# Attention's second product with the values' two halves side by side in one stationary operand

## The reference, cut to what matters

```
proj = rmsnorm(x) @ w_in            # sparse q,k,v | indexer | stick-breaking q,k,v | gates
o_a  = sparse attention             # 8 heads of 64: top-128 keys by the indexer, T5 bias, softmax
o_b  = stick-breaking attention     # 8 heads of 64, strictly causal
m    = sigmoid(gate_a) * (o_a @ W_a) + sigmoid(gate_b) * (o_b @ W_b)
x    = x + rmsnorm(m @ w_out);  x = x + rmsnorm(SwiGLU(rmsnorm(x)) @ w_down)
```

## Time and profile before

| | us |
|---|---|
| median of 3 runs | 823.9 (822.6 to 826.22) |
| the profiled execution | 822.08 |
| its span, first to last instruction | 820.3 |
| PE busy | 798.2 |
| DVE, ACT, POOL busy | 383.6, 325.7, 406.0 |

### The profile page before, as it was taken

The page is one execution under the profiler, slowest core; times in us unless marked ns, Lnnn a source line. Parts: engine busy times, 40 slices in busy tenths (PEclk is TensorE's granted clock), DMA queues, the critical chain, the costliest instruction groups (busy, mean ns, idle before and its releaser), DMA issues.

```text
span 820.3 us, 10762 instructions
## 1 busy us (share of the span) xinstructions
PE 798.2 (97%) x3822; PEld 663.4 (81%) x3822; DVE 383.6 (47%) x539; ACT 325.7 (40%) x472; POOL 406.0 (49%) x246
## 2 busy tenths in 40 slices
PE   6999999999999899999999999999999999999996
PEld 5887888888888788788878988888888888888885
DVE  4359996687686766349707300000000020444464
ACT  5463322656656565543136322222222232232242
POOL 4276464544476867434455234444444443443462
PEclk9999999999999999999999999999999999999999
DMA  7323333223222222223267033233333332232212
GB/s 221 101 52 94 138 116 102 68 58 81 52 54 63 58 59 78 64 78 102 103 219 218 1 101 84 81 92 102 102 102 102 102 102 80 74 102 102 102 52 103
DMA packets 103913, 77.29 MB, mean 94 GB/s; under 512 B 3777, under 2 KB 95945, under 8 KB 103882
## 3 DMA queue, kind: packets, MB, share of 16 engines
q1 hardware_dynamic: 103882, 76.87, 31.6%
HBM read 74.75 MB, written 3.68 MB: 96 GB/s over the span
## 4 chain that ended last, share of the span: by engine, by line
PE 90%; DMA 3%; ACT 2%; DVE 1%; issue 1%; POOL 1%; SPq 0%; ACTq 0%; POOLq 0%
PE ps L435 20%; PE ps L407 20%; PE ps L409 20%; PE ps L408 19%; PE ps L628 4%; PE ps L617 2%; DMA raw<-in_w_gate_up 2%; PE ps L598 1%; PE ps L596 1%; DMA raw<-in_w_in 1%; POOL w_lo L1044 1%; DMA raw<-in_w_out 1%; ACT w_hi L738 1%; DVE h_lo L1188 0%; PE ps L527 0%
## 5 line engine op out<-in xcount | busy, mean ns | idle before, releaser
L1044 POOL TENSOR_TENSOR w_lo<-raw,w_hi 128x1024 fp32r<-128x1024 f32 x116 | 281.9, 2430 | 341.6 <-ACT w_hi L738 312.2
L407 PE MATMUL ps<-h_hi,w_hi 128*128 128x512 f32 (+1 forms) x656 | 252.7, 385 | 8.9 <-issue 3.0
L738 ACT ACTIVATE w_hi<-raw 128x1024 fp32r<-128x1024 f32 (+1 forms) x111 | 117.6, 1059 | 338.5 <-PE ps L409 229.0
L409 PE MATMUL ps<-h_hi,w_lo 128*128 128x512 f32 (+1 forms) x656 | 249.2, 380 | 0.0
L408 PE MATMUL ps<-h_lo,w_hi 128*128 128x512 f32 (+1 forms) x656 | 248.7, 379 | 0.0
L407 PEld LDWEIGHTS ps<-h_hi,w_hi 128*128 128x128 f32 x656 | 123.5, 188 | 32.8 <-issue 4.9
L409 PEld LDWEIGHTS ps<-h_hi,w_lo 128*128 128x128 f32 x656 | 123.4, 188 | 24.1
L408 PEld LDWEIGHTS ps<-h_lo,w_hi 128*128 128x128 f32 x656 | 123.6, 188 | 21.3
L1421 DVE TENSOR_TENSOR act<-silu,ps 128x512 f32 (+1 forms) x22 | 15.1, 688 | 211.2 <-PE ps L409 211.2
L1426 DVE TENSOR_TENSOR d_lo<-act,d_hi 128x512 fp32r<-128x512 f32 x18 | 43.2, 2404 | 54.1 <-ACT d_hi L986 54.1
L435 PE MATMUL ps<-w_lo,d_hi 128*128 128x512 f32 x144 | 45.4, 396 | 0.0
(11 more groups left out here) (179 smaller groups left out, 1216.4 us busy)
## 6 DMA issues: line engine op xcount, KB each, us to landing
raw<-in_w_in SPq DMA_DIRECT2D x44, 512.0 KB, 4.8
raw<-in_w_gate_up SPq DMA_DIRECT2D x44, 512.0 KB, 4.9
raw<-in_w_down SPq DMA_DIRECT2D x22, 512.0 KB, 3.9
raw<-in_w_out SPq DMA_DIRECT2D x8, 512.0 KB, 3.9
x_in<-in_x SPq DMA_DIRECT2D x4, 512.0 KB, 5.7
raw<-in_w_branch_sb SPq DMA_DIRECT2D x8, 256.0 KB, 3.1
raw<-in_w_branch_sparse SPq DMA_DIRECT2D x8, 256.0 KB, 3.2
x<-in_x SPq DMA_DIRECT2D x4, 512.0 KB, 8.2
```

Source lines behind the costliest of these rows:

```text
L407: mm(acc, whi_c, a_hi_, start=first, stop=False)
L409: return mm(acc, wlo_c, a_hi_, start=False, stop=last)
L738: run(w_hi[:, at(u), :], raw[:, at((d % 2) * 2 + u), :], ACT.Copy).then_inc(w_hi_done, 1)
L1044: nc.gpsimd.tensor_tensor(w_lo[:, at(u), :], raw[:, at((d % 2) * 2 + u), :], w_hi[:, at(u), :], sub).then_inc(w_lo_done, 1)
```

## The change

The two heads of a pair get a stationary operand each, 128 wide: the 64 columns of the head's `v_hi`, and beside them the 64 of its `v_lo` (`v_both[:, head, block, :]`). Two passes, over `a_hi` and over `a_lo`, give `v_hi`·a in PSUM rows 0 to 63 and `v_lo`·a in rows 64 to 127. (The product lo·lo, left out before, is now included.) The result of the head is the sum of the two parts. ScalarE copies the lower part to SBUF, to the rows where the head's result does not belong (`out_rest`), VectorE adds the upper part from PSUM into the rows where it does (`sum_out`), and from there `out_hi` and `rest_out` make the halves.

The order changes with it. `turn_probs(i+1)` waits for `out_summed` of head i. `out_hi(i-1)` stands behind `turned_hi(i)` on ScalarE. `rest_out(i-1)` stands ahead of `sum_out(i)` on VectorE. `out_rest(i)` on ScalarE stands where `out_hi(i)` stood and, because `out_parts` has one buffer, waits for `o_lo_done` of head i-1 too. Two small tiles move to memory that is used otherwise later.

```
@@ attend, on TensorE
-                for p, (v, pr) in enumerate(((v_hi, a_hi), (v_hi, a_lo), (v_lo, a_hi))):
-                    ins = mm(z(1, k * P, S), v[:, k, :], pr[:, a:a + n],
-                             start=k == 0 and p == 0, stop=k == TB - 1 and p == 2, skip_group_check=True)
+                for p, pr in enumerate((a_hi, a_lo)):
+                    ins = mm(z(1, k * P, S), v_both[:, i % 2, k, :], pr[:, a:a + n],
+                             start=k == 0 and p == 0, stop=k == TB - 1 and p == 1, skip_group_check=True)
@@ turn_probs
-                pe.wait_ge(o_lo_done, i)
+                pe.wait_ge(out_summed, i)
@@ split_v: the same number of elements, now in runs of 64
-            run(v_hi[:, :, :], v_tok[:, :, first:first + P], ACT.Copy).then_inc(v_hi_done, 1)
+            run(v_both[:, :, :, 0:HD], v_tok[:, :, first:first + P].rearrange("p t (h d) -> p h t d", h=2),
+                ACT.Copy).then_inc(v_hi_done, 1)
@@ ScalarE
+        def out_rest(i):
+            r = slice(HD * (i % 2), HD * (i % 2) + HD)
+            sc.wait_ge(out_done, i + 1)
+            other = slice(HD - r.start, P - r.start)
+            if i:
+                sc.wait_ge(o_lo_done, i)
+            run(out_parts[other, :], ps[HD:P, 5, :], ACT.Copy).then_inc(out_rest_done, 1)
         def out_hi(i):
-            sc.wait_ge(out_done, i + 1)
-            run(o_hi[r:r + HD, chunk, :], ps[r:r + HD, 5, :], ACT.Copy).then_inc(o_hi_done, 1)
+            sc.wait_ge(out_summed, i + 1)
+            run(o_hi[r, chunk, :], out_parts[r, :], ACT.Copy).then_inc(o_hi_done, 1)
@@ ScalarE, step i
             turned_hi(i)
+            if i:
+                out_hi(i - 1)
...
-            out_hi(i)
+            out_rest(i)
...
+        out_hi(ALL - 1)
@@ VectorE
+        def sum_out(i):
+            r = slice(HD * (i % 2), HD * (i % 2) + HD)
+            ve.wait_ge(out_rest_done, i + 1)
+            other = slice(HD - r.start, P - r.start)
+            tt(out_parts[r, :], ps[0:HD, 5, :], out_parts[other, :], ALU.add).then_inc(out_summed, 1)
         def rest_out(i):
-            tt(o_lo[r, chunk, :], ps[r, 5, :], o_hi[r, chunk, :], sub).then_inc(o_lo_done, 1)
+            tt(o_lo[r, chunk, :], out_parts[r, :], o_hi[r, chunk, :], sub).then_inc(o_lo_done, 1)
@@ VectorE, step i
-            rest_out(i)
+            if i:
+                rest_out(i - 1)
+            sum_out(i)
+        rest_out(ALL - 1)
```

More of the change, by code:

```diff
@@ L149, in build @@
     rel_t = sb("rel_t", BUCKETS, rows=HEADS)
-    f_bias = sb("f_bias", 384, rows=HEADS)
-    zeros8 = sb("zeros8", 384, rows=HEADS)
     zone1 = top[0]
@@ L165, in build @@
     q_lo = sb("q_lo", [2, S], F32R)
-    v_hi, v_lo = sb("v_hi", [TB, P], F32R), sb("v_lo", [TB, P], F32R)
+    v_both = sb("v_both", [2, TB, P], F32R)
+    out_parts = sb("out_parts", S)
     bias_mask = sb("bias_mask", TRI)
@@ L185, in build @@
     tri_f = sb("tri_f", [2, P])
+    f_bias, zeros8 = sb("f_bias", 384, rows=HEADS), sb("zeros8", 384, rows=HEADS)
     top[0] = zone1
@@ L252, in build @@
     out_done, o_hi_done, o_lo_done = sems("out_done", "o_hi_done", "o_lo_done")
+    out_rest_done, out_summed = sems("out_rest_done", "out_summed")
     ends_done, keep_done, beta_done, scan_done = sems("ends_done", "keep_done", "beta_done", "scan_done")
@@ L884, in turned_hi @@
             run(a_hi[:, :], z(1, 0, TRI), ACT.Copy).then_inc(a_hi_done, 1)
+        def out_rest(i):
[5 more added lines that the diff above has]
+            run(out_parts[other, :], ps[HD:P, 5, :], ACT.Copy).then_inc(out_rest_done, 1)
         def out_hi(i):
-            r, chunk = HD * (i % 2), (i // 2 + PAIRS) % KC
-            sc.wait_ge(out_done, i + 1)
-            run(o_hi[r:r + HD, chunk, :], ps[r:r + HD, 5, :], ACT.Copy).then_inc(o_hi_done, 1)
+            r, chunk = slice(HD * (i % 2), HD * (i % 2) + HD), (i // 2 + PAIRS) % KC
+            sc.wait_ge(out_summed, i + 1)
+            run(o_hi[r, chunk, :], out_parts[r, :], ACT.Copy).then_inc(o_hi_done, 1)
         def gate(slot):
@@ L1058, in split_v @@
             first = (g * P + W) % (2 * W)
-            nc.gpsimd.tensor_tensor(v_lo[:, :, :], v_tok[:, :, first:first + P], v_hi[:, :, :], sub).then_inc(v_lo_done, 1)
+            nc.gpsimd.tensor_tensor(v_both[:, :, :, HD:P], v_tok[:, :, first:first + P].rearrange("p t (h d) -> p h t d", h=2),
+                                    v_both[:, :, :, 0:HD], sub).then_inc(v_lo_done, 1)
         def bias_and_mask(j):
```

## The result

The changed kernel took 840.87 us (median of 6 runs, 835.94 to 842.7), the kernel before 824.33 in the same session (6 runs, 820.97 to 826.97): 1.0179 times as long, 95% interval 1.0145 to 1.0213, some 15 us slower. The profiled execution took 835.94 (span 834.2), 13.9 more than the 822.08 of before. It is the quickest of the six: four of them took 840.8 to 842.7, at a mean clock of 0.983 to 0.985 against its 0.993, so the profile shows less of the loss than the median. The prediction had 3.9 slower and a range that ended at 833. Its sign holds, and its mechanism in the stick-breaking half; its account of the softmax half and its size do not.

The account below looks back on a forecast made before the run. TensorE, busy 97%, bounds the kernel; after the change ScalarE and VectorE bound the stick-breaking half. 3.2 + 0.7 = 3.9 us slower: 822.1 becomes 826.0, as median 827.8; own range 825 to 831, wider range 815.5 to 833.

Parts of the forecast that it names:

- Its sign: Whole kernel: slower, by 3.9 us; chance of measurably slower 0.41, same 0.39, faster 0.20.
- The pass removed: TensorE's attend: one of three passes gone, 0.62 us a head, 10.0 us in all for 16.
- The operations added: Per head, one more ScalarE copy of 0.59 us and one more VectorE add of 0.69; 9.4 and 11.0 in all.
- rest_out's contention: VectorE's rest_out, now with two SBUF inputs, contends with GpSimd: 0 to 2.2 us a head, taken as 0.4.
- The loop: Stick-breaking half: out_rest(i) waits for rest_out(i-1) behind VectorE's step; five turns 62.45 us plus 2.0, a_hi(6) at 238.6.
- Tile 12: TensorE's gate after a_hi(6), through GpSimd's w_lo: TensorE goes on at 250.4, 3.2 us later than before.
- The softmax half: Later heads: longer chains to the tiles' gates offset attends saved; 0.7 us lost, bounds 1.3 gained to 2.5 lost.
- the loop binds in both halves: Rival: softmax loops take 12.2 us in place of 11.3, 5.4 more; 9 slower in all, 833; chance 0.16.
- Behind the stage: After the last attend: four operations in place of two, about 5 us, under 8 pieces of 0.7; free.
- the ring: The wait of ScalarE's out_rest(i) for VectorE's rest_out(i-1), forecast at 62.45 us plus 2.0 for five stick-breaking turns.

Follow-up runs that it names:

- experiment 3: The changed kernel with a third pass (a_lo repeated) in each attend: 840.65 us, ratio 1.0190.
- kernel 2: The changed kernel with rest_out(i-1) ahead of turned_lo on VectorE and out_hi(i-1) ahead of the tiles and turned_hi on ScalarE: 826.68 us, ratio 1.0011.
- kernel 4: The kernel before without the pass v_lo times a_hi and with none of the added work: 823.36 us, ratio 0.9964.
- kernels 1: The changed kernel with rest_out(i-1) moved right behind turned_lo(i) on VectorE: 827.6 us, ratio 0.9983.
- experiment 5: The changed kernel with rest_out(i-1) right behind turned_lo(i) for i under 8 only (stick-breaking heads): 829.62 us, ratio 1.0029.
- 6: The changed kernel with rest_out(i-1) right behind turned_lo(i) for i from 8 on only (softmax half): 834.69 us, ratio 1.0074.
- 7: The changed kernel with spare matmuls in TensorE's waits ahead of tiles 12, 16, 19 and 22: 838.26 us, ratio 1.0122.
- 9 to 12: Spare matmuls in waits of kernel 4 (0.9919), kernel 2 (0.9969), the kernel before (0.9998); last, kernel 2 with some, w_lo first in steps 6 and 13 (0.9895).
- 8: kernel 2 with GpSimd's w_lo ahead of bias and mask in steps 6, 8, 9, 11 and 13: 824.53 us, ratio 0.9972.

## Why the prediction was right in sign and wrong in size

**The pass removed** (10.0, of which 6.2 was held to show): the shortest attends in the chain of waits after are these,

```profile
258.66 1.21 PE ps L629 x8
```

0.66 less than the earlier trace rows, where 0.62 was taken. What of it shows at the gates was right too, 6.7 measured against 6.2, but only with the clock kept. As it runs, 3.0 remain. In the changed kernel itself nothing remains (experiment 3).

**The operations added** (0.59 and 0.69): 0.594 and 0.683. Right. rest_out's contention, taken as 0.4 a head, came out uneven: 0.68 or 0.69 for heads 0 to 4, 1.11 or 1.12 for heads 5 to 10 (0.42 over), then 0.99, 0.68, 2.90, 0.68 and 2.35. (The row beside the Trainium skill's rule in the prediction, 2.50 for the cast, is of an instruction with one input; the row for two inputs in SBUF is k_both's 0.68 to 2.89 in the earlier trace rows.) The operations together, with the loop cut, cost 0.5%, some 4 us, by kernels 2 and 4, 0.2% by 1 and 4; the prediction had no price for them outside the loop and the gates' longer chains.

**The loop.** From a_hi(1) to a_hi(6) the starts after are 173.56, 187.40, 199.50, 213.35, 224.83, 238.83: loops of 13.84, 12.10, 13.85, 11.48 and 14.00, 65.3 in all, where 62.45 + 2.0 = 64.4 was worked out. The prediction's terms give 13.60, 9.85, 13.58, 11.48 and 13.94. The one that differs is the loop of step 2, 2.25 longer: in the earlier trace rows the cast and k_both had no GpSimd instruction in their way; after, they take 1.41 and 2.88. A term read off one trace as undisturbed was undisturbed by its position only. a_hi(6) came at 238.83 against 238.6.

**Tile 12.** TensorE went on at 250.87 against 250.4, 3.7 later than before's 247.19, where 3.2 was forecast (4.3 by the common start, as the stage began earlier). Right in mechanism and nearly in size. It was not priced that the clock falls behind this wait, another 1.7 us.

**The softmax half: the step that failed.** It was put at 0.7 lost, on the ground that the banks are freed by as many operations as before and turn_probs "gains or loses nothing there as long as neither is late". From tile 12 to the end of the stage it lost 12.1 - 4.3 = 7.8. Sum_out was late. The timelines of DVE and ACT in step 8 of the changed kernel:

```profile
275.28 1.12 DVE L1357 TENSOR_TENSOR o_lo<-out_parts,o_hi 64x512 fp32r<-64x512 f32 x1
...
276.49 0.59 ACT L895 ACTIVATE out_parts<-ps 64x512 f32<-64x512 f32 x1 [2.83 <-DVE o_lo L1357]
277.12 0.68 DVE L1351 TENSOR_TENSOR out_parts<-ps,out_parts 64x512 f32<-64x512 f32 x1 [0.72 <-ACT out_parts L895]
```

rest_out, out_rest, sum_out, and 0.15 us behind its end the turn_probs of step 9, at 277.95, that had waited 1.70; again 1.60 and 1.04 in steps 11 and 12, 4.3 us of new waits on TensorE. The prediction had followed the loop only to a_hi; it has a second way out, over the bank that sum_out frees. The rival *the loop binds in both halves*, at 9 slower, was nearer; experiment 5 puts the price of the second half's loop at 3.8 us alone, near the 5.4 given for it, though within wide bounds. That the two halves together cost 5 us more than apart is likely and not shown.

**The term that is missing: the granted clock.** Every wait was counted once. Twice the share of clock missing, times the span, is an estimate of the time spent at 1.2 GHz: 8.3 to 8.9 us on the mean of the runs before (0.995), 21.8 on the mean of the runs after (0.987), 9.2 with the gaps filled. Thirteen us more at half speed hold work of 6.5 at full speed; the filling gave 4.7 back. No step of the prediction contained it. In the profiled execution the second half divides as shown above, 8.2 us of new idle time and 5.1 of low clock against 5.6 saved. How the 16 us of the medians divide stays open, since filling also alters when the gates open.

**Behind the stage** (put at nothing; +2.5). TensorE is busy there for 457.1 us in both kernels. At 457.37 it waited 2.41 us for VectorE's y_buf, which had taken 3.50 us beside GpSimd's wu_lo, where the same instruction took 1.28 before (there wu_lo stood beside it too, and it was wu_lo's two instructions that were long, 6.11 us in place of 4.96):

```profile
453.82 3.50 DVE L1198 SCALAR_TENSOR_TENSOR y_buf<-x,rstd,g_ffn_row 128x1024 f32<-128x1024 f32 x1
```

This is not the ring. The same wait, 4.0 to 4.5 us long and with a low clock behind it each time, stands in eight other profiled executions (kernels 1, 2, 6, 7 and 9 to 12), the kernel before with its waits filled among them; in the kernel before, 4 and 5 it is missing, in 3 and 8 it is 0.2. Two profiled executions can so differ by some 4 us, and the clock behind it, for a reason that is not the edit. What decides it was not shown.

## What to carry to other kernels

When a result is staged through one buffer, write down which instruction frees it, what stands ahead of that instruction in its engine's queue, and what stands behind the new wait on the other engine: if that closes a ring, add up one turn of it and compare it with the bounding engine's step, in each kind of step, and follow every way out of the ring, the banks it frees included. Here one such 0.69 us operation behind VectorE's long work cost 2%, and moving it cost nothing. And work taken from the bounding engine in front of a gate turns into a longer wait, which can lower its clock; so price a saved matmul by what the gates let through, then look at the clock behind each wait that grows.

## What the runs showed of the hardware that was not expected

Spare matmuls in a wait brought the time down: 0.9964 to 0.9919 where waits of 1.2 to 2.9 us stood ahead of five tiles, 1.0011 to 0.9969 in kernel 2, 1.0179 to 1.0122 where those ahead of tiles 12, 16 and 22 were 3.3 to 4.1 (each pair's intervals overlap a little, and all three moved alike); and nothing, 1.0000 to 0.9998, in the kernel before, whose waits at tiles 12 and 16 were 1.02 and 2.29 and whose windows behind them had a clock of 1.00. TensorE's clock behind a wait was 0.50 in the window at 283 to 287 of kernel 4, where the wait at tile 16 was 2.93 us, and the same matmul took 0.77 us in place of the 0.47 in kernel 4 filled.

The length of the wait alone does not say whether the clock falls. In kernel 2 a wait of 2.13 us ahead of tile 12 and one of 2.87 ahead of tile 16 went the other way round, by the windows behind them:

```profile
242.00:247.00 5.00, 4.11 (x16) 3.66 (x17) 3.62 (x5) 1.01 (x2) 3.11 (x2) 0.66 0.15 30
282.00:288.00 6.00, 5.61 (x30) 4.80 (x31) 3.54 (x3) 2.86 (x8) 4.32 (x3) 1.00 0.07 9
```

In kernel 3 a wait of 2.95 us ahead of tile 12 left the clock at 1.00 too. So a wait that grows can cost the clock, and the profile of each kernel has to be read for it.
